# Fourteen blocks of split fp32r products given other shapes in one decoder layer on one Trainium2 core

## The reference, cut to what matters

```python
xn = rmsnorm(x, g_mix)                       # 264 x 2048
z = xn @ w_in                                # u, v, p, q and three gates of 2048 columns each
merged = (sigmoid(gate_0) * (br_a @ w_br_a) + sigmoid(gate_1) * (br_b @ w_br_b)
          + sigmoid(gate_2) * (br_c @ w_br_c))
h = x + merged @ w_o                         # 2048 x 2048
```

## Time and profile before

| What | us |
|---|---|
| median of 2 runs (1585.43 to 1587.51) | 1586.47 |
| the profiled execution, its own time | 1585.38 |
| its span, first to last instruction | 1583.6 |
| mean granted TensorE clock, as a share of full speed | 0.928 |

### The profile page before, as it was taken

How to read it: one execution, slowest core, us unless ns; L and a number is a source line. 1 busy time by engine, 2 the same in 40 slices (tenths; PEclk the granted TensorE clock), 3 DMA queues, 4 the chain that set the end, 5 groups by cost and what they waited for, 6 DMA issues and landing times.

```text
span 1583.6 us, 24065 instructions
## 1 busy us (share of the span) xinstructions
PE 1349.8 (85%) x9971; PEld 920.1 (58%) x9971; DVE 556.1 (35%) x898; ACT 407.4 (26%) x623; POOL 19.9 (1%) x54
## 2 busy tenths in 40 slices
PE   9999999999999999999778578488487497497597
PEld 8999999999999999963222232232232232232231
DVE  6657765554455555432112012012021021021024
ACT  6545343333333344332102002002002002002003
POOL 0000000000000000010000000000000000000000
PEclk9999999999999999999989789789789699699699
DMA  9777445545555669799999999999999999999997
GB/s 364 291 273 280 158 160 187 186 159 193 180 184 185 260 235 388 283 398 427 437 433 440 432 426 441 432 427 442 432 428 440 430 430 439 430 430 439 427 430 301
DMA packets 42425, 544.68 MB, mean 344 GB/s; under 512 B 5753, under 2 KB 7929, under 8 KB 13697
## 3 DMA queue, kind: packets, MB, share of 16 engines
q1 hardware_dynamic: 42088, 543.96, 83.8%
q10 hardware_dynamic: 288, 0.04, 0.0%
HBM read 540.30 MB, written 3.68 MB: 343 GB/s over the span
## 4 chain that ended last, share of the span: by engine, by line
PE 69%; DMA 28%; ACT 1%; DVE 1%; issue 0%; SPq 0%; ACTq 0%; DVEq 0%
DMA ring<-in_expert_chunks 28%; PE bank L1653 12%; PE bank L1654 12%; PE bank L1655 12%; PE bank L2125 8%; PE bank L2122 6%; PE bank L2039 5%; PE bank L1980 3%; PE bank L2025 1%; ACT side L1087 1%; PE bank L2031 1%; PE bank L1972 1%; PE bank L2115 1%; PE bank L2027 1%; PE bank L1912 1%
## 5 line engine op out<-in xcount | busy, mean ns | idle before, releaser
L1142 DVE TENSOR_TENSOR w_lo<-ring,w_hi 128x1024 fp32r<-128x1024 f32 x216 | 255.9, 1226 | 224.8 <-ACT w_hi L845 224.2
L1653 PE MATMUL bank<-xn_hi,w_hi 128*128 128x264 f32 x1120 | 319.0, 285 | 0.0
L1654 PE MATMUL bank<-xn_lo,w_hi 128*128 128x264 f32 x1120 | 317.3, 283 | 0.0
L1655 PE MATMUL bank<-xn_hi,w_lo 128*128 128x264 f32 x1120 | 317.1, 283 | 0.0
L845 ACT ACTIVATE w_hi<-ring 128x1024 fp32r<-128x1024 f32 x216 | 217.1, 1052 | 373.6 <-PE bank L1655 313.9
L2122 PE MATMUL bank<-side 128*32 128x512 f32 x1024 | 131.4, 651 | 97.0 <-DMA side<-in_expert_chunks 96.8
L1653 PEld LDWEIGHTS bank<-xn_hi,w_hi 128*128 128x128 f32 x1120 | 210.9, 188 | 1.7 <-issue 1.4
L1654 PEld LDWEIGHTS bank<-xn_lo,w_hi 128*128 128x128 f32 x1120 | 211.1, 188 | 0.1
L1655 PEld LDWEIGHTS bank<-xn_hi,w_lo 128*128 128x128 f32 x1120 | 210.0, 187 | 0.0
L2122 PE MATMUL bank<-ring,side 128*32 128x512 f32 x752 | 102.4, 667 | 86.4 <-DMA ring<-in_expert_chunks 86.4
L1553 DVE TENSOR_SCALAR side<-bank,small 128x128 f32<-128x128 f32 x56 | 19.6, 351 | 369.7 <-PE bank L1980 369.7
(11 more groups left out here) (333 smaller groups left out, 1581.5 us busy)
## 6 DMA issues: line engine op xcount, KB each, us to landing
ring<-in_dense_units SPq DMA_DIRECT2D x108, 1024.0 KB, 4.8
ring<-in_expert_chunks SPq DMA_DIRECT2D x21, 4096.0 KB, 22.5
trunk<-in_expert_chunks SPq DMA_DIRECT2D x13, 4096.0 KB, 35.0
ring<-in_expert_chunks SPq DMA_DIRECT2D x20, 2048.0 KB, 16.2
ring<-in_expert_chunks SPq DMA_DIRECT2D x17, 1024.0 KB, 18.2
side<-in_expert_chunks SPq DMA_DIRECT2D x4, 4096.0 KB, 29.6
side<-in_expert_chunks SPq DMA_DIRECT2D x5, 2048.0 KB, 11.3
trunk<-in_expert_chunks SPq DMA_DIRECT2D x5, 2048.0 KB, 16.3
```

The source lines that it names most:

```text
L1142: V.tensor_tensor(w_lo[n % 2][:, js, :], raw[n % 2][:, js, :], w_hi[n % 2][:, js, :], ALU.subtract).then_inc(lo_done, 1)
L1653: mm(ps[:, 0:n], w_hi[b][:, j, :], x_hi[:, j, :], start=j == k0, stop=False)
L1654: mm(ps[:, 0:n], w_hi[b][:, j, :], x_lo[:, j, :], start=False, stop=False)
L1655: ins = mm(ps[:, 0:n], w_lo[b][:, j, :], x_hi[:, j, :], start=False, stop=j == k1 - 1)
```

## The change

Fourteen of the blocks issue their products in another shape; what they sum up for the 264 wanted columns is the same. Six ways occur, in the first group of gates (u = 1 to 5) and in the output projection (k = 2 to 10):

- `wide_products`, u = 1, 2, 3 with n = 272, 280, 288 and k = 2, 3, 4, 5 with n = 272, 280, 288, 320: each matmul of j = 0 to 14 streams n columns instead of 264 (the surplus are the next values in the tile; what they add up to is not read). The row j = 15 keeps 264.
- `column_products`, u = 4 with the cut at 136, k = 6 at 248, k = 7 at 136: each matmul is done as two, over columns 0 to cut and cut to 264.
- `operand_products`, u = 5, k = 8: inside each half of 8 rows, all `w_hi` with `x_hi` first, then all `w_hi` with `x_lo`, then all `w_lo` with `x_hi`. k = 9 does so with rows in the order 0, 4, 1, 5, 2, 6, 3, 7.
- `ordered_products`, k = 10: the three matmuls of a row together as before, with the rows in that order.

```diff
+            def wide_row(x, j, n):
+
+                return x[:, j, 0:T] if n == T or j == KT - 1 else x[:, j:j + 2, :].rearrange("p j t -> p (j t)")[:, 0:n]
+
+            def wide_mg(part, j, n):
+
+                if n == T or j == KT - 1:
+                    return mg[:, j, part, :]
+                return mg[:, j:j + 2, :, :].rearrange("p j s t -> p (j s t)")[:, part * T:part * T + n]
+
+            def wide_products(ps, b, x_hi, x_lo, lo, n):
+
+                for j in range(KT):
+                    if j % (KT // PIECES) == 0:
+                        pe.wait_ge(lo[0], lo[1] + (j * PIECES // KT + 1 - PIECES))
+                    m = T if j == KT - 1 else n
+                    mm(ps[:, 0:m], w_hi[b][:, j, :], x_hi(j, n), start=j == 0, stop=False)
+                    mm(ps[:, 0:m], w_hi[b][:, j, :], x_lo(j, n), start=False, stop=False)
+                    ins = mm(ps[:, 0:m], w_lo[b][:, j, :], x_hi(j, n), start=False, stop=j == KT - 1)
+                return ins
+
+            def column_products(ps, b, x_hi, x_lo, lo, cut):
+
+                for j in range(KT):
...
+                    for c0, c1 in ((0, cut), (cut, T)):
+                        mm(ps[:, c0:c1], w_hi[b][:, j, :], x_hi[:, j, c0:c1], start=j == 0 and c0 == 0, stop=False)
+                    for c0, c1 in ((0, cut), (cut, T)):
+                        mm(ps[:, c0:c1], w_hi[b][:, j, :], x_lo[:, j, c0:c1], start=False, stop=False)
+                    for c0, c1 in ((0, cut), (cut, T)):
+                        ins = mm(ps[:, c0:c1], w_lo[b][:, j, :], x_hi[:, j, c0:c1], start=False, stop=j == KT - 1 and c1 == T)
+                return ins
+
+            def operand_products(ps, b, x_hi, x_lo, lo, order):
+
+                half = KT // PIECES
+                for q in range(PIECES):
+                    pe.wait_ge(lo[0], lo[1] + (q + 1 - PIECES))
+                    js = [q * half + i for i in order]
+                    for w, x in ((w_hi, x_hi), (w_hi, x_lo), (w_lo, x_hi)):
+                        for j in js:
+                            ins = mm(ps[:, 0:T], w[b][:, j, :], x[:, j, :], start=q == 0 and w is w_hi and x is x_hi and j == js[0],
+                                     stop=q == PIECES - 1 and w is w_lo and j == js[-1])
+                return ins
+
+            def ordered_products(ps, b, x_hi, x_lo, lo, order):
...
+            def first_gates(u):
+                pe.wait_ge(z_done, Z_G + u - 1)
...
+                if u in (1, 2, 3):
+                    ins = wide_products(bank[b], b, wide(xn_hi), wide(xn_lo), lo, T + 8 * u)
+                elif u == 4:
+                    ins = column_products(bank[b], b, xn_hi, xn_lo, lo, 136)
+                else:
+                    ins = operand_products(bank[b], b, xn_hi, xn_lo, lo, range(KT // PIECES))
+                ins.then_inc(z_ready, 1)
...
             for u in range(1, 6):
-                gates(0, u)
+                first_gates(u)
...
             for k in range(K_JOINT):
-                three_products(z(Z_O + k), k % 2, mg_hi, mg_lo, 0, KT, lo_after(N_OUT + k),
-                               beside(k)).then_inc(z_ready, 1)
+                ps, b, lo = z(Z_O + k), k % 2, lo_after(N_OUT + k)
+                if k in (2, 3, 4, 5):
+                    ins = wide_products(ps, b, high, low, lo, (272, 280, 288, 320)[k - 2])
+                elif k in (6, 7):
+                    ins = column_products(ps, b, mg_hi, mg_lo, lo, (248, 136)[k - 6])
+                elif k == 8:
+                    ins = operand_products(ps, b, mg_hi, mg_lo, lo, range(KT // PIECES))
+                elif k == 9:
+                    ins = operand_products(ps, b, mg_hi, mg_lo, lo, (0, 4, 1, 5, 2, 6, 3, 7))
+                elif k == 10:
+                    ins = ordered_products(ps, b, mg_hi, mg_lo, lo, (0, 4, 1, 5, 2, 6, 3, 7))
+                else:
+                    ins = three_products(ps, b, mg_hi, mg_lo, 0, KT, lo, beside(k))
+                ins.then_inc(z_ready, 1)
```

More of the change, by code:

```diff
@@ new lines, in ordered_products @@
+            def ordered_products(ps, b, x_hi, x_lo, lo, order):
+                half = KT // PIECES
+                for q in range(PIECES):
+                    pe.wait_ge(lo[0], lo[1] + (q + 1 - PIECES))
+                    for i in order:
+                        j = q * half + i
+                        mm(ps[:, 0:T], w_hi[b][:, j, :], x_hi[:, j, :], start=q == 0 and i == order[0], stop=False)
+                        mm(ps[:, 0:T], w_hi[b][:, j, :], x_lo[:, j, :], start=False, stop=False)
+                        ins = mm(ps[:, 0:T], w_lo[b][:, j, :], x_hi[:, j, :], start=False, stop=q == PIECES - 1 and i == order[-1])
+                return ins
@@ L1850, in pooled @@
                     mm(mid[half:P, 0:T], block[1, 2][:, half:P], d[2], start=False, stop=True).then_inc(aux_ready, 2)
+            def first_gates(u):
+                pe.wait_ge(z_done, Z_G + u - 1)
+                b, lo = u % 2, lo_after(N_Z + u)
+                wide = lambda x: lambda j, n: wide_row(x, j, n)
+                if u in (1, 2, 3):
[5 more added lines that the diff above has]
+                ins.then_inc(z_ready, 1)
             def gates(g, u):
@@ L1895, in _ @@
             pe.wait_ge(x_zero, 1)
+            high, low = (lambda j, n: wide_mg(0, j, n)), (lambda j, n: wide_mg(1, j, n))
             for k in range(K_JOINT):
-                three_products(z(Z_O + k), k % 2, mg_hi, mg_lo, 0, KT, lo_after(N_OUT + k),
-                               beside(k)).then_inc(z_ready, 1)
+                ps, b, lo = z(Z_O + k), k % 2, lo_after(N_OUT + k)
[12 more added lines that the diff above has]
+                ins.then_inc(z_ready, 1)
             for u in range(JOINT):
```

## The result

The changed kernel takes 1605.24 us (median of 1604.93 and 1605.54) against 1586.47: ratio 1.0121, 95% interval 1.0104 to 1.0137. The forecast was 1604.3, in a range of 1595 to 1610, within 2%. The profiled execution took 1604.93 us, its span is 1603.2.

A forecast was written before the change was run, and what follows sets the result against it. TensorE was taken to bound the dense stage and the weight stream the expert stage, delays passing on fully. Wide 2.9 + column 14.9 + order 0 = 17.8 us on 1585.4, plus 1.1 for the median, gave 1604.3 us, range 1595 to 1610.

The forecast's parts named there:

- Dense time is a sum of distances: Dense stage, up to about 670 us: TensorE bounds it, so its time sums matmul start distances, 120.8 to 121.7 ns each.
- the 2.3 us by which the engines are ahead: Dense stage: the engines that prepare the next unit are 2.3 us ahead of TensorE, and longer blocks make that more.
- A delay reaches the end: Expert stage: DMA waits on things that follow TensorE, so a delay before 670 us passes on one to one.
- The rival that the expert stream takes up the projection's part: Expert weight stream starts on its own, so only the gates' 5.9 us would count: 1592.4 us; chance 0.04.
- Column blocks, 112 ns a matmul, 14.9 us: u = 4, k = 6, 7: weight-load floor of 112 ns a matmul adds 4.95, 5.06 and 4.91 us, together 14.9.
- The bound of 128 ns from the gather rows: Column blocks, upper bound: 128 ns a matmul, from 12 gather matmuls of 128 columns, adding 19.0 us in sum.
- The rival of a cheap second load: Column blocks: the fp32r load hides behind a short matmul, costing 1.4 us; 1590.8, or up to 1597; chance 0.14.
- Wide blocks, 2.9 us: u = 1 to 3, k = 2 to 5: extra streamed columns add 0.92 us in gates and 1.99 us in projection.
- the upper bound of 3.5: Wide blocks: a line from 256 to 512 columns, 0.418 ns a column, gives 1.25 and 2.26 us, 3.5 in all.
- a line from 264 to 512 columns gives ... 0.428 ns a column: Wide blocks: price of an extra column, (227.0 - 120.8) / 248 = 0.428 ns in gates, 0.425 in projection.
- Order blocks, nothing: u = 5, k = 8, 9, 10: same 48 matmuls of 264 columns, cost nothing; bound 0.3 us for the four.
- The clock's rival: Column blocks: granted clock falls to 1.2 GHz, distances near double, 29 us more, 1633 us; chance 0.05.

The follow-up runs named there:

- e4: All ten output projection blocks k = 2 to 11 cut at column 136, gates as in the kernel before; 1635.29 us, ratio 1.0316.
- e1: Only the three column blocks (u = 4, k = 6, k = 7) keep their new shape, against the kernel before; 1600.55 us, ratio 1.0095.
- e5: Probe on the kernel before: k = 2 to 10 with fewer weight columns or other column ranges, some outputs left out; 1611.47 us, only block times count.
- e6: Probe on the kernel before: k = 2 to 10 stream other widths, 192 to 512 columns, with full weights; 1597.43 us, only block times count.
- e3: Only the four order blocks (u = 5, k = 8, 9, 10) keep their new shape, against the kernel before; 1585.95 us, ratio 1.0002.
- e7: Only k = 6 and 7 changed from the kernel before, 264 columns cut into three parts of 88; 1633.40 us, ratio 1.0298.
- e8: Only k = 6 and 7 changed from the kernel before, 264 columns cut into 248, 8 and 8; 1632.41 us, ratio 1.0291.

## Why the prediction was right, point by point

- *Dense time is a sum of distances.* Right: the blocks' sum is 18.2 us and the expert stage starts 18.2 us later. Two readings on the way were rougher than they sound. The digit of PE stays at 9 up to the 19th slice, 752 us, not the 17th; what marks the expert stage from 670 us on is the DMA digit. And the 2.3 us by which the engines are ahead hold for the gates. In the projection before, a unit could be late, and its `w_lo` was then complete at 638.99 for a block that began at 640.08, 1.1 us ahead. PE waited in neither case.

```profile
635.53 2.01 ACT L845 ACTIVATE w_hi<-ring 128x1024 fp32r<-128x1024 f32 x2 [4.55 <-DMA ring<-in_dense_units]
636.63 2.36 DVE L1142 TENSOR_TENSOR w_lo<-ring,w_hi 128x1024 fp32r<-128x1024 f32 x2 [1.76 <-ACT w_hi L845]
```

- *A delay reaches the end.* Right, by the way that it named: the queue's waits for `w_lo` grew with the blocks, and e4 shows it with a lever of 49 us. The rival that the expert stream takes up the projection's part is out by e1 and e4.
- *Column blocks, 112 ns a matmul, 14.9 us.* Right: 111 to 112 ns, 14.7 us. The fp32 rows with nearly nothing to stream gave the fp32r load's price, and e5 shows that the load's columns set it. k = 6 was taken apart rightly too: 226 ns a pair, where e6 has 114.7 ns for 248 columns and e4 111.7 for a load. The bound of 128 ns from the gather rows was too high for fp32r. The rival of a cheap second load is out, and so is the 81 ns a matmul that the Trainium skill (TensorE: Matmul & The Clock Gate, Back-to-back issue gap) gives for 128 columns: in these blocks the trace disagrees, with 111 ns.
- *Wide blocks, 2.9 us.* The mechanism was right, the term too small: 3.3 us, near the upper bound of 3.5. The failing step is "a line from 264 to 512 columns gives ... 0.428 ns a column". Its far end was a row of other work, in which the weights stream, at 227.0 ns; 512 columns of `mg` take 231.1 (e6). With the slope of e6 the gates would cost 45 x 48 x 0.441 = 0.95 us and the projection 2.06, against 1.14 and 2.17 measured. In the gates the near end adds 0.1 us: 120.8 ns lies 0.9 below the line of e6, and the wide gates lie on it (128.8 and 132.8 ns at 280 and 288 columns, where the line gives 128.8 and 132.3). In `mg` the distances are 125.9, 129.4, 133.2 and 146.3 ns, where 124, 128, 131 and 145 were forecast; that 272 to 288 columns lie 0.6 to 0.9 ns above the line is not explained. The upper bound took 264 for a lucky width, from 256 columns of another operand at 120.0 ns; 256 columns of `mg` take 117.9 (e6), on the line, so it isn't one.
- *Order blocks, nothing.* Right: 0.03 us for the four by themselves (e3); the 0.15 in the changed kernel is mostly the first matmul behind a column block, as e1 shows. That nothing is saved by a repeated load is shown by the column blocks, not by these.
- *The clock's rival.* It didn't happen in the changed kernel, and e4 held clock 1.00 for 107 us of blocks cut in two. But the mechanism exists, one cut further: e7 is 3.0% slower. No row of before could tell that two parts are safe and three are not, so that this change stayed on the safe side is in part luck. The price given, a factor of 1.9, came out: 213 / 111.7 = 1.9. The reason given against it (short and long matmuls mix at clock 1.00) doesn't hold in general, as e8 mixes them too.
- *The sum.* The wide blocks came out 0.4 us dearer than forecast, the column blocks 0.2 cheaper and the order blocks 0.15 dearer. These partly cancel, and with the 0.6 us outside the blocks the median is 0.9 us above the forecast.

## What to carry to other kernels

In this kernel each matmul carries its own load, with new weights or the same, and costs the larger of its load and its stream. 128 fp32r weight columns cost 111 ns and N streamed columns 5.3 + 0.441 N ns, so they meet near 240 columns. A part narrower than that pays for a full load. A part wider than that pays for its columns almost in proportion: from 264 to 320, 21% more, the distance grew by 20%, from 121.7 to 146.3 ns. Price such a change by the distances of starts, not by durations, and before cutting a block finer look at the granted clock of a run of several microseconds of just that shape, since a busy PE row alone doesn't show that it holds.

## What the runs showed that was not expected

- With the clock at its lower level (1.2 GHz) a matmul bound by the load of 128 columns takes 213.3 ns, against 111.7 at full clock (both in e7). So the load slows with the clock as the stream does (264 columns: 220 against 121.7 ns).
- In k = 6 of the changed kernel the starts alternate, 198 ns from a 248-column matmul to the 16-column one and 28 ns from that to the next, though the pair takes 226 ns, one stream of 248 columns and one load. The start of one matmul in a record says little, the period says it all.
